# Second block of a two-block kernel: part of its f32 products computed from high and low parts, and the query norms moved ahead

## What is computed

```python
hc = ctx * (1.0 + mod_c[1]) + mod_c[0]           # 256 context tokens
hx = x * (1.0 + sc_a) + sh_a                     # 256 tokens of the sequence
side = hc @ w_in[:, OFF_XBC:]                    # context: inner inputs, dt, keys, values
proj = hx @ w_in                                 # z, q, inner inputs (xbc), dt, k, v
xbc = silu(depthwise_conv5(xbc_raw) + conv_b)
dt = softplus(dt_raw + dt_bias)
y_ssd = two scans over chunks of 128 tokens (forward and backward), gated by silu(z), rms-normed
q, k = rope(rms_norm(q)), rope(rms_norm(k))      # 16 query heads, 4 key heads, 64 wide
o = softmax(q @ k^T / 8) @ v                     # over context and sequence
mix = concat([y_ssd, o]) @ w_out                 # 2048 -> 1024
x = layer_norm(alpha * x + g_a * mix)
x = layer_norm(alpha * x + g_f * experts(x * (1.0 + sc_f) + sh_f))    # 16 experts of width 256
```

## Time and profile before

| | |
|---|---|
| time, median of 3 runs | 1807.83 us (1807.72 to 1809.81) |
| the profiled execution | 1803.91 us, span of its instructions 1801.8 us |
| TensorE busy | 93% of the span |
| VectorE, ScalarE, GpSimd busy | 61%, 42%, 14% |
| DMA | 157 GB/s on average |
| mean granted TensorE clock | 0.957 |
| second block | from 1072.6 us of the span; experts from 1487.1 us |

### The profile page before, as it was taken

How to read it: one execution, slowest core, us unless ns; L and a number is a source line. 1 busy time by engine, 2 the same in 40 slices (tenths; PEclk the granted TensorE clock), 3 DMA queues, 4 the chain that set the end, 5 groups by cost and what they waited for, 6 DMA issues and landing times. The chain is left out here.

```text
span 1801.8 us, 26601 instructions
## 1 busy us (share of the span) xinstructions
PE 1674.2 (93%) x10712; PEld 1375.3 (76%) x10712; DVE 1090.2 (61%) x1496; ACT 760.5 (42%) x1069; POOL 250.6 (14%) x287
## 2 busy tenths in 40 slices
PE   7999999899989999999899989998989968999996
PEld 5887889799978888888799864444566437999995
DVE  4669997566655669896566530376557244455555
ACT  4365554455444465545455421213127123334431
POOL 0200004144210200012243200011220000000000
PEclk9999999899999999999899999999879988999998
DMA  6545455465553545535465553222000222455551
GB/s 256 193 182 190 166 183 187 170 244 218 188 202 140 211 164 188 188 140 196 164 237 212 188 194 140 70 93 71 29 19 1 94 93 94 150 180 184 186 186 70
DMA packets 40121, 282.07 MB, mean 157 GB/s; under 512 B 4816, under 2 KB 5072, under 8 KB 6864
## 3 DMA queue, kind: packets, MB, share of 16 engines
q1 hardware_dynamic: 38432, 273.15, 41.8%
q10 hardware_dynamic: 1584, 7.42, 1.1%
HBM read 279.50 MB, written 1.05 MB: 156 GB/s over the span
## 5 line engine op out<-in xcount | busy, mean ns | idle before, releaser
L429 DVE TENSOR_TENSOR ring_low<-ring,sb_hi 128x2048 fp32r<-128x2048 f32 x116 | 271.2, 2338 | 183.7 <-ACT sb_hi L424 183.5
L424 ACT ACTIVATE sb_hi<-ring 128x2048 fp32r<-128x2048 f32 x116 | 222.5, 1918 | 279.6 <-DMA ring<-weights 121.8
L578 PE MATMUL psum<-sb_hS,sb_hi 128*128 128x256 f32 x704 | 202.9, 288 | 9.6 <-DVE ring_low L429 9.4
L1844 DVE TENSOR_TENSOR sb_split<-ring,sb_split 128x2048 fp32r<-128x2048 f32 x48 | 109.9, 2292 | 153.7 <-ACT sb_split L1839 153.7
L581 PE MATMUL psum<-sb_hS,sb_hi 128*128 128x256 f32 x704 | 199.5, 283 | 0.0
L582 PE MATMUL psum<-sb_hS,ring_low 128*128 128x256 f32 x704 | 198.9, 283 | 0.0
L840 PE MATMUL psum<-sb_hfT,ring_low 128*128 128x256 f32 x704 | 198.6, 282 | 0.0
L2158 PE MATMUL psum<-sb_hfS,sb_split 128*128 128x256 f32 x512 | 146.6, 286 | 6.0 <-DVE sb_hfS L2700 3.9
L578 PEld LDWEIGHTS psum<-sb_hS,sb_hi 128*128 128x128 f32 x704 | 134.0, 190 | 19.9 <-DVE ring_low L429 12.8
L2162 PE MATMUL psum<-sb_hfS,sb_split 128*128 128x256 f32 x512 | 146.0, 285 | 0.0
L2161 PE MATMUL psum<-sb_hfS,sb_split 128*128 128x256 f32 x512 | 146.0, 285 | 0.0
(11 more groups left out here) (392 smaller groups left out, 3863.2 us busy)
## 6 DMA issues: line engine op xcount, KB each, us to landing
ring<-weights SPq DMA_DIRECT2D x256, 1024.0 KB, 4.8
sb_rows_ffn<-rows ACTq DMA_DIRECT2D x4, 512.0 KB, 4.5
sb_rows_mix<-rows ACTq DMA_DIRECT2D x2, 1024.0 KB, 7.4
sb_rows<-rows ACTq DMA_DIRECT2D x1, 2048.0 KB, 9.1
sb_x<-x_in SPq DMA_DIRECT2D x2, 512.0 KB, 6.2
sb_y<-ctx_in SPq DMA_DIRECT2D x1, 1024.0 KB, 6.2
out<-sb_x SPq DMA_DIRECT2D x2, 512.0 KB, 2.7
sb_const<-const SPq DMA_DIRECT2D x1, 711.0 KB, 13.7
```

The lines of the kernel that those rows point to most:

```text
L424: act.activation(hi_of(n), ring[:, c % SLOTS, :], ACT.Copy).then_inc(hi_ready, 1)
L429: eng.tensor_tensor(low_of(n), ring[:, SPLIT_CHUNKS[n] % SLOTS, :], hi_of(n).bitcast(F32), ALU.subtract).then_inc(lo_dve, 1)
L578: mm = pe.matmul(out, hi[:, k, bs], hS[:, 0, k, :], start=(k == 0), stop=False)
L1844: dve.tensor_tensor(split[:, n % SPLITS, 1, :], ring[:, (first_moe + n) % SLOTS, :], split[:, n % SPLITS, 0, :].bitcast(F32), ALU.subtract ...
```

## The change

In the second block, chunks 2 to 11 (queries' second half, keys and values, inner inputs) and 16 to 23 (output projection) are now used as high and low parts, as the experts' are. z (12 to 15) and the queries' first half (0 and 1) stay f32.

- `weight_hi` (ScalarE) writes a chunk's high part into one of two places for the input chunks, `w_z` and the second half of `w_probs`, or one of two for the projection, `w_q` and the first half of `w_probs`. From the third chunk on it waits until the chunk two before is used. `weight_lo` (VectorE) writes the low part into `ring_low`, at the chunk's slot. TensorE waits for `w_lo`.
- `hT` gets a high copy (`in_high`, ScalarE, 4 instructions for each source) and a low one (`in_low`, VectorE, 4 for each source). The attention's output is drained twice, to a high and a low part; the scan's output is copied high by ScalarE and subtracted by VectorE (4 instructions each).
- TensorE transposes the context after the queries' first half, and makes the second half after it.
- `q_norm(0)` and `q_norm(1)` run on VectorE after the low part of chunk 5 and before that of chunk 6 and the dt chain. `k_norm` runs after the state weights, ahead of L2545's products. GpSimd's roots follow this order: the two of the queries, then the keys'.
- ScalarE makes the high parts of chunks 16 and 17 in pairs 11 and 13 of the attention, VectorE the low parts in pairs 12 and 14.

The core of the diff:

```diff
+MEM2_MIX_SPLIT = [("_a", (6144,)), ("h_high", (KD, 512)), ("_b", (2048,)), ("mix_low", (16, T)), ("_c", (2048,)), ("w_q", (CH,)), ("_d", (1024,)),
+                  ("w_probs", (2 * CH,)), ("h_low", (KD, 512))]
+IN_SPLIT, OUT_SPLIT = list(range(2, 12)), list(range(16, 24))
...
-        if s == 1:
-            for c in range(2):
-                for t in range(TT):
-                    jobs.plan(("q", c, t))
+        for t in range(TT):
+            jobs.plan(("q", 1 - s, t))
...
+    def weight_hi(act, n):
+
+        i, c = SPLIT_ORDER.index(n), first + n
+        if i >= 2 and n - 2 in SPLIT_ORDER:
+            act.wait_ge(used[(c - 2) % SLOTS], (c - 2) // SLOTS + 1)
+        act.wait_ge(landed[c % SLOTS], (c // SLOTS + 1) * 16)
+        act.activation(w_place(n), ring[:, c % SLOTS, :], ACT.Copy).then_inc(w_hi, 1)
+
+    def weight_lo(dve, n):
+
+        dve.wait_ge(w_hi, SPLIT_ORDER.index(n) + 1)
+        c = (first + n) % SLOTS
+        dve.tensor_tensor(ring_low[:, c, :], ring[:, c, :], w_place(n).bitcast(F32), ALU.subtract).then_inc(w_lo, 1)
...
+            def tokens_split(tiles, names):
+
+                for half in range(2):
+                    hi, lo = (w.rearrange("p (k n) -> p k n", k=4) for w in next_parts())
...
+                            mm = pe.matmul(jobs.out(name), hS[0][:, kk, ts], hi[:, k, :], start=(kk == 0), stop=False)
+                            if k == 0:
+                                carry(mm)
+                            pe.matmul(jobs.out(name), hS[0][:, kk, ts], lo[:, k, :], start=False, stop=False)
+                            mm = pe.matmul(jobs.out(name), hS[1][:, kk, ts], hi[:, k, :], start=False, stop=(kk == KD - 1))
...
                 for k in range(KD):
-                    mm = pe.matmul(jobs.out(("xbc", b)), chunk[:, k, b % 2 * P:(b % 2 + 1) * P], hT[:, k, :], start=(k == 0), stop=(k == KD - 1))
+                    mm = pe.matmul(jobs.out(("xbc", b)), hi[:, k, fs], hS[0][:, k, :], start=(k == 0), stop=False)
                     if k == 0:
                         carry(mm)
+                    pe.matmul(jobs.out(("xbc", b)), hi[:, k, fs], hS[1][:, k, :], start=False, stop=False)
+                    mm = pe.matmul(jobs.out(("xbc", b)), lo[:, k, fs], hS[0][:, k, :], start=False, stop=(k == KD - 1))
...
+            for i in range(2, 8):
+                if i == 6:
+                    for v in range(2):
+                        for c in range(2):
+                            copy_out(("gB", v, c), gB[:, v, c * 512:(c + 1) * 512])
+                weight_hi(act, OUT_SPLIT[i])
...
+            for s in (1, 0):
+                for c in range(2):
+                    scale_in(("in", s, c, 0), hT[:, 4 * c:4 * c + 4, 2 * s * P:(2 * s + 1) * P], 8 + 4 * c, 4 * c, 1 - s)
+                in_low(s)
+                if s == 1:
+                    weight_lo(dve, 2)
+                    weight_lo(dve, 3)
+            weight_lo(dve, 4)
+            weight_lo(dve, 5)
+            dve.wait_ge(params, 32)
+            q_norm(0)
+            q_norm(1)
+            weight_lo(dve, 6)
+            jobs.wait_filled(dve, "dt")
...
             for b in range(DX):
+                if b % 2 == 0 and b < DX - 2:
+                    weight_lo(dve, 7 + b // 2)
                 taps(b)
-                if b == 2:
-                    k_norm()
-                if b in (5, 8):
-                    q_norm((b - 5) // 3)
```

More of the change, by code:

```diff
@@ L1915, in strip_sums, with next_parts @@
                 jobs.fill(mm, name)
+            def next_parts():
+                n = state["chunk"] - first
+                state["chunk"] += 1
+                pe.wait_ge(w_lo, SPLIT_ORDER.index(n) + 1)
+                return w_place(n), ring_low[:, (first + n) % SLOTS, :]
+            def tokens_split(tiles, names):
+                for half in range(2):
+                    hi, lo = (w.rearrange("p (k n) -> p k n", k=4) for w in next_parts())
+                    for tile, name in zip(tiles, names):
+                        if half == 0:
+                            jobs.claim(pe, name)
+                        ts = slice(tile * P, (tile + 1) * P)
+                        for k in range(4):
+                            kk = 4 * half + k
+                            mm = pe.matmul(jobs.out(name), hS[0][:, kk, ts], hi[:, k, :], start=(kk == 0), stop=False)
[3 more added lines that the diff above has]
+                            mm = pe.matmul(jobs.out(name), hS[1][:, kk, ts], hi[:, k, :], start=False, stop=(kk == KD - 1))
+                        if half == 1:
+                            jobs.fill(mm, name)
+                    if half == 0:
+                        done_with(mm)
+                    else:
+                        owe()
             def tokens(kind, tiles, names, halves=(0, 1)):
@@ L1947, in _ @@
                             jobs.wait_drained(pe, ("in", 1, c, t))
[L1948 to L1949 removed]
+                    tokens("q", (2, 3), [("q", 0, t) for t in range(TT)])
+                else:
+                    pe.wait_ge(in_lo, 4)
+                    tokens_split((2, 3), [("q", 1, t) for t in range(TT)])
             pe.wait_ge(params, 32)
@@ L2334, in _ @@
                     weighted_out(*divmod(n // 4 - 1, 2))
+                if n in (11, 13):
+                    if n == 11:
+                        for d in range(2):
+                            jobs.wait_filled(act, ("yo", 1, 1, d))
+                    weight_hi(act, OUT_SPLIT[(n - 11) // 2])
             for g in range(2):
@@ L2630, in _, with weighted_low @@
             gather_y(*UNITS[-1][:2])
+            def weighted_low(t, h):
+                region_, _, before, _ = jobs.jobs[("O", t, h)]
+                dve.wait_ge(drained[region_], before + 1)
+                jobs.drain(dve.tensor_tensor(mix_low[:, 8 + 4 * h:12 + 4 * h, t * P:(t + 1) * P], jobs.out(("O", t, h)).rearrange("p (b t) -> p b t", b=4),
+                                             mix_o[:, 4 * h:4 * h + 4, t * P:(t + 1) * P].bitcast(F32), ALU.subtract), ("O", t, h))
             for n in range(len(PAIRS)):
@@ L2687, in out_source @@
                 return wait, jobs.out(name), done
+            for i in range(4, 8):
+                weight_lo(dve, OUT_SPLIT[i])
             for n in range(2):
```

166 lines of the change are left out of this document (110 added, 56 removed).

## The result

The changed kernel takes 1783.6 us (median of four runs, 1781.5 to 1785.7) against 1807.8 us for the kernel before beside it (1807.1 to 1809.8): a ratio of 0.9863 with a 95% interval of [0.985, 0.9875], so 24.2 us faster. The forecast was 1786.2 us, between 1775 and 1797. Run again later beside other kernels, it took 1785.9 us, ratio 0.9875 [0.9859, 0.9892]. The profiled execution took 1781.5 us with a span of 1779.5 us, where the one of before took 1803.9 and 1801.8: 22.4 us.

What follows compares the result with a forecast made beforehand. TensorE, busy for 93% of the span at a nearly full clock, was taken to bound the kernel. The terms summed to -21.6 us from the 1807.8 us median, giving 1786.2 us; forecast 1781 to 1791, range 1775 to 1797.

Steps and rivals of the forecast that it cites:

- Products: Second block's 208 products on TensorE: three parts at 0.684 us replace f32 at 0.860 us; -36.6 us.
- Two waits that go: TensorE's waits before the dt strips (-1.8 us) and after the inner inputs (-1.0 us) go or shrink.
- The stall: Before the first inner input TensorE waits for chunk 6's low part, behind both query norms on VectorE; +8.8 us.
- The clock behind it: After that idle TensorE's products run at half clock for a while; +2.5 us, between 0 and 6.8.
- The key norm and GpSimd: Key norm after the taps, slowed beside GpSimd, delays the states TensorE waits on; +1.5 us, between 0 and 1.7.
- Attention: High and low parts made in pairs 11 to 14 exceed ScalarE's and VectorE's idle; +2.9 us, between 0 and 6.1.
- Last low part: Attention output's last low part stands ahead of four products that TensorE waits for; +0.7 us.
- Residual: At the projection's end VectorE must finish two expert low parts before the residual; +1.4 us.
- Hand-overs: Output projection: handing over a place takes 4.2 us, hidden under 5.5 us of products; 0, up to 6 us.
- Rival (c): Inner inputs and projection: the two places work as one, opening all hand-overs; +46 us, 1832 us; chance 0.06.
- Rival (b): Waits in attention, states and projection add 5 to 13 us; 1791 to 1800 us, chance 0.18.

Runs made afterwards that it cites:

- the doubled copy: Changed kernel with ScalarE making each of the last six high parts of the output projection twice; 1788.87 us, ratio 0.9893.
- two more moves: Key norm in pieces between taps, chunk 7's parts ahead of the dt chain; with chunk 6's low part inside the second query norm, on the changed kernel: 1773.98 us.
- the 7.3 us of one edit: Changed kernel with chunk 6's low part made inside the second query norm's wait for GpSimd; 1778.58 us, ratio 0.9842.
- the 8.7 of another: Changed kernel with the key norm cut into four pieces between the taps of tiles 2, 4, 6 and 8; 1777.25 us, ratio 0.9831.

## Why the prediction was right, point by point

- **Products, -36.6.** Right in kind, a little large. Keys and values: 22.23 us for 96 records, 0.232 a record, so 0.695 us a product in parts where I took 0.684. The inner inputs (69.5 us from 1135.50 to 1205.02, less 2.8 lost to the clock, 288 records) give 0.232 too. 208 x (0.860 - 0.695) is 34.3, which is 2.3 less. I took the low end of my spread; the prediction named -35 for 0.231.
- **Two waits that go, -1.8 and -1.0.** 1.79 and 1.16.
- **The stall, +8.8.** 8.22, with the same queue, releaser and place; moving one low part out from behind the norms removed it.
- **The clock behind it, +2.5.** From 1135.50 to 1141.1 the products went at half speed: 2.8.
- **The key norm and GpSimd, +1.5.** The price was right and the consequence wrong. The contention is there: L2555 took 4.84 us beside GpSimd's two products (L2987, 4.18 us from 1218.28), and the norm 15.0 us in all, from 1212.38. The same instruction took 1.42 us between the taps, in the kernel with the key norm in pieces (L2585, last row).

```profile
1218.24 4.84 DVE L2555 TENSOR_TENSOR sb_kv<-sb_kv,sb_sm 128x256 f32<-128x256 f32 x4 [3.38 <-POOL sb_sm L2971]
1223.12 1.43 DVE L2559 TENSOR_TENSOR sb_kv<-sb_kv,sb_rows 128x256 f32<-128x256 f32 x4
...
1227.70 1.22 DVE L2658 TENSOR_TENSOR sb_xdt<-sb_xs,sb_sm 128x1024 f32<-128x1024 f32 x1 [0.32 <-PE psum L1987]
```

```profile
1177.15 1.42 DVE L2585 TENSOR_TENSOR sb_kv<-sb_kv,sb_sm 128x256 f32<-128x256 f32 x4
```

  But the stretch is 0.2 us longer than before in one profile and 1.2 shorter in the other, at a higher clock (0.89 and 0.90 for 0.86), with 6.9 and 6.5 us of TensorE idle for 6.0, and cutting the norm out of it left 6.9. The step that failed is the last: that what exceeds VectorE's idle reaches TensorE one to one. The norm ended at 1227.4 us, and TensorE was in gate products (L1987) beyond that, up to 1230.62. The first wait in the states is 2.28 us for 1.52 in the first profile, 1.46 in the second.
- **Attention, +2.9.** 1.4 by the windows of before and after, 1.9 by taking the projection's parts out. ScalarE's first high part cost 0.90 where I took 1.35, and the low part at pair 12, which I put at 1.6, cost 0.24: that is the term that was too large. I counted the idle of one pair as all the room there is.
- **Last low part, +0.7.** 0.8 (2.33 for 1.56 of idle). **Residual, +1.4.** 1.3 (6.64 for 5.35).
- **Hand-overs, 0.** 0; the doubled copy shows the 1.2 us of margin. Rival (c), two places acting as one, is excluded by that run. Rival (b) is by the windows: no wait in the projection and 1.7 us in the attention, where it wanted 5 to 13.
- **Missing: the clock in the units, +4.7.** And half clock once in the projection (49.7 us at 0.97, against 48.2 at 1.00 in the second profile). I had looked at the clock only behind the stall. The prediction calls it nearly full everywhere, but that line has a 7 and several 8s, and the units stood at 0.79 before the change.

The sum of the terms as measured in the first profile is -34.3 - 1.8 - 1.2 + 8.2 + 2.8 + 0.2 + 1.4 + 0.8 + 1.3 + 4.7 + 1.5 = -16.4, against 15.8 us by which its second block is shorter. In the second profile the block is 19.8 us shorter. The forecast had 21.6 for it. The time was nevertheless 2.6 us under the forecast (0.3 in the second measurement), since the medians differ by more than the profiles' second blocks do: the kernel before stands 3.9 us over its own profiled execution, the changed one 2.1 over the first and not at all over the second. Where the 3.9 us lie isn't known, as no other execution of the kernel before was profiled. So a part of the good agreement is luck: the second block gained less than the sum said, by the half clock that no term had, and the spread outside it made up for that.

## What to carry to other kernels

When a step is moved on an engine, ask what is queued behind it and who waits for that; this walk gave the 8.2 us to within 0.6, and showed the repair. With two more moves and the gate projection one unit later the kernel takes 1771.4 us, where the change itself takes 1783.6 or 1785.9. A delay on one engine costs only what the engine that waits for it can't spend on other work: the key norm's was hidden under gate products. And check what filling a wait does to the engine that ends it. Before a gain of a few us is credited to an edit, compare the granted clock of stretches that the edit doesn't touch: here the units moved by 8 us, and held 5.5 of the 7.3 us of one edit and 7.7 of the 8.7 of another.

## What was unexpected of the hardware

- TensorE's clock fell to half for 27.3 us in one piece while it was busy for all of it (27.21 us, 104 records), in the same place in eight of thirteen profiles of the changed kernel and its relatives, and for 10.2 us or less at a time in that place in the others. The units took 68.4 to 76.2 us with the same work. What decides between the two isn't settled. 5.6 us more of work ahead doesn't, in two kernels. Moving the gate products by one unit took the stretch away, in two kernels; so did edits that lie 50 us and more ahead of it, in ways that I can't tell in advance.
- A GpSimd operation on 128x16 numbers took 2.09 us instead of 0.20 because VectorE was in an operation of 2.28 us on SBUF.
